# Token blocks of 144, 64 and 32 per weight quarter in a mixture-of-experts stage

## The reference, cut to what matters

```python
logits = jnp.einsum('btd,de->bte', h, router_w) + router_b
top_v, top_i = lax.top_k(logits, TOP_K)                # 2 of 8 experts
gates = jax.nn.softmax(top_v, axis=-1)
for e in range(N_EXPERTS):                             # D = 1024, expert width 3584
    y = y + combine[..., e:e+1] * (silu(h @ wg[e]) * (h @ wu[e])) @ wd[e]
```

## Time and profile before

| | |
|---|---|
| median of 3 runs | 2012.54 us (2012.41 to 2013.05) |
| profiled execution | 2011.59 us, of it 2009.7 us span |
| TensorE busy | 88% of the span |
| mean granted TensorE clock | 0.91 |
| SyncE's DMA queue | 65.1% of 16 engines' span |

### The profile page before, as it was taken

One profiled execution on the slowest core, in us unless ns is written; L12 is line 12 of the kernel. 1 busy time (PEld: TensorE's weight loads), 2 busy tenths in 40 slices (PEclk: granted clock), 3 DMA queues, 4 the chain that ended last, 5 costly groups with the idle time before them and its releaser, 6 DMA issues.

```text
span 2009.7 us, 27189 instructions
## 1 busy us (share of the span) xinstructions
PE 1771.1 (88%) x10676; PEld 1294.9 (64%) x10677; DVE 429.1 (21%) x810; ACT 241.5 (12%) x489; POOL 168.4 (8%) x204
## 2 busy tenths in 40 slices
PE   6999875566789999967889999999999999999874
PEld 3766443555567777745339689788777887778331
DVE  2023436764211111375000000000000000000102
ACT  2122342111110000132000000001000010000101
POOL 4002204562000000040000000000000000000001
PEclk8998597666889999977999999999999999999997
DMA  9762041001745554530898878879999999999995
GB/s 345 268 228 88 2 127 56 1 1 27 261 156 210 209 189 158 191 133 2 312 391 327 302 252 319 299 255 354 363 345 345 347 348 352 343 348 364 371 392 206
DMA packets 233583, 481.58 MB, mean 240 GB/s; under 512 B 14383, under 2 KB 89011, under 8 KB 233123
## 3 DMA queue, kind: packets, MB, share of 16 engines
q1 hardware_dynamic: 228027, 471.85, 65.1%
q0 software_dynamic: 3920, 5.44, 0.9%
q10 hardware_dynamic: 1568, 3.34, 0.5%
HBM read 473.06 MB, written 7.90 MB: 239 GB/s over the span
## 4 chain that ended last, share of the span: by engine, by line
PE 78%; DMA 6%; DVE 6%; POOL 4%; issue 3%; ACT 2%; SPq 1%; ACTq 0%; POOLq 0%; DVEq 0%
PE bank L1108 76%; DMA ring<-in_moe_w_up 4%; POOL ring L2305 2%; DMA ring<-in_ada_w 1%; POOL other L2317 1%; ACT ring L1590 1%; DVE wide L1882 1%; SPq L2396 0%; DVE wide L1866 0%; PE bank L1241 0%; DVE wide L2208 0%; SPq L2423 0%; PE bank L714 0%; DMA ring<-in_cache_fox_logf 0%; PE bank L1366 0%
## 5 line engine op out<-in xcount | busy, mean ns | idle before, releaser
L1108 PE MATMUL bank<-wide,ring 128*128 128x144 f32 (+4 forms) x4240 | 695.5, 331 | 16.6 <-DVE wide L1878 9.3
L1108 PEld LDWEIGHTS bank<-wide,ring 128*128 128x128 f32 (+2 forms) x4240 | 616.1, 190 | 100.6 <-issue 32.5
L1108 PE MATMUL bank<-ring 128*64 128x512 f32 (+8 forms) x1748 | 340.5, 521 | 50.1 <-DMA ring<-in_moe_w_up 24.1
L1108 PE MATMUL bank<-other,ring 128*128 128x144 f32 (+3 forms) x2016 | 291.4, 319 | 53.5 <-POOL ring L2305 31.1
L1108 PEld LDWEIGHTS bank<-other,ring 128*128 128x128 f32 (+1 forms) x2016 | 267.1, 192 | 78.2 <-POOL ring L2305 32.4
L1108 PEld LDWEIGHTS bank<-ring 128*64 128x64 f32 (+4 forms) x1748 | 144.7, 158 | 225.4 <-issue 188.4
L1108 PE MATMUL bank<-ring,other 128*64 128x512 f32 x560 | 128.0, 596 | 8.4 <-ACT other L747 8.4
L820 DVE TENSOR_TENSOR other<-other,bank 64x512 f32<-64x512 f32 (+1 forms) x40 | 24.5, 613 | 442.1 <-ACT other L744 442.1
L838 DVE TENSOR_TENSOR other<-other,bank 128x288 f32<-128x288 f32 (+3 forms) x48 | 21.4, 446 | 350.9 <-PE bank L1108 324.6
L2375 POOL TENSOR_TENSOR small<-const 128x1 f32<-128x1 f32 x1 | 0.2, 193 | 1075.8 <-DMA expert_rows<-ring 1075.8
L1108 PEld LDWEIGHTS bank<-ring,other 128*64 128x64 f32 x560 | 38.4, 137 | 75.4 <-issue 64.3
(11 more groups left out here) (354 smaller groups left out, 961.6 us busy)
## 6 DMA issues: line engine op xcount, KB each, us to landing
ring<-in_moe_w_gate SPq DMA_DIRECT2D x32, 2048.0 KB, 7.9
ring<-in_moe_w_up SPq DMA_DIRECT2D x32, 2048.0 KB, 12.7
ring<-in_moe_w_down SPq DMA_DIRECT2D x32, 2048.0 KB, 16.9
ring<-in_ada_w SPq DMA_DIRECT2D x24, 2048.0 KB, 13.5
ring<-in_moe_w_gate SPq DMA_DIRECT2D x32, 1536.0 KB, 11.1
ring<-in_moe_w_up SPq DMA_DIRECT2D x32, 1536.0 KB, 14.8
ring<-in_moe_w_down SPq DMA_DIRECT2D x32, 1536.0 KB, 16.5
ring<-in_w_in SPq DMA_DIRECT2D x5, 2048.0 KB, 12.6
```

Of the source, the lines that this page charges most:

```text
L1108: return pe.matmul(out, lhsT, rhs, start=start, stop=stop, skip_group_check=True)
```

## The change

- **Blocks.** An expert of up to 240 tokens (`CAP`) is cut into at most three blocks: one of 144 if it has over 96, one of 64 if over 32 remain, one of 32 for what is then left. Here: expert 2 is 144 + 32, expert 3 is 144, expert 4 is 64 + 32, expert 1 is 32, and 0, 5, 6, 7 are 64 each. The 192-wide form is gone. All blocks of an expert use one and the same loaded weight quarter.
- **Turns.** The plan has one word per quarter of an expert (a turn, `TURNS` = 40, of them 32 alive). Every engine loops over turns in batches of eight, reads the word and branches to the blocks. Waits count blocks (`b`), so a place is free for the next turn when the last block of this one is done with it.
- **The 32-token block.** Four column groups of 32: up and gate of part 0 in groups 0 and 1, then up and gate of part 1 in groups 2 and 3; then all seven transposes, then down over all four groups.
- **Pairs.** Now heavies are paired with experts of up to 96 tokens; the order of experts comes out as before.
- **Tokens** are copied by ScalarE per block and turn. **Rows** of a heavy expert are transposed in its own last turn. **Stores** move to GpSimd's queue. Of expert 0 only the first quarter is issued ahead of the plan.
- **Planner.** `moe_plan` has 19 small vector operations more and, for the turns, 11 operations on 40 x 10 elements; `moe_orders` (18 operations without data) runs ahead of the router's result.

```diff
-CAP, MID, HALF = 192, 144, 64
+MID, HALF, QUART = 144, 64, 32
+CAP, LIGHT = MID + HALF + QUART, HALF + QUART
...
+        def quarter_block(pe, mm, R, b):
...
+            pe.wait_ge(s("xe_ready"), b + 1)
+            pe.wait_ge(*after("moe_act", 5 * b - 2))
+            for part in range(2):
+                w = P * PARTS[part][1]
+                for kind in ("gate", "up"):
+                    pe.wait_ge(loaded(kind, part), 16 * R + 16)
+                for c in range(DC):
+                    for half, kind in enumerate(("up", "gate")):
+                        m = mm(B[0][group(2 * part + half), 0:w], xe_quart[:, c, :], moe_tile(kind, part)[:, c, :], c == 0, c == DC - 1)
+                        if c == DC - 1:
+                            m.then_inc(s(f"moe_{kind}"), 2)
+            pe.wait_ge(*after("moe_act", 5 * b + 3))
+            for part, (j0, n) in enumerate(PARTS):
+                o = group(2 * part)
+                for j in range(n):
+                    m = mm(B[TURN + part][:, QUART * j:QUART * (j + 1)], ea[o, part, P * j:P * (j + 1)], ident[o, o], True, True)
+                m.then_inc(s("moe_turn"), 1)
+            pe.wait_ge(*after("moe_silu", 6 * b + 6))
+            for part, (j0, n) in enumerate(PARTS):
+                pe.wait_ge(loaded("down", part), 16 * R + 16)
+                w = moe_tile("down", part)
+                for j in range(n):
+                    for p in range(2):
+                        m = mm(B[TURN + 1][group(2 * (j % 2) + p), :], eaT_few[:, j0 + j, 0:QUART], w[:, j, 512 * p:512 * (p + 1)],
+                               j0 + j < 2, j0 + j >= SUBS - 2)
...
+            act.wait_ge(*after("moe_up", 4 * b))
+            act.activation(xe_quart, xall[:, :, bass.ds(at, QUART)], ACT.Copy).then_inc(s("xe_ready"), 1)
...
-                    sp.wait_ge(*after("moe_down", 2 * R - 1 + part))
+                    sp.wait_ge(*after("moe_down", 2 * b - 1 + part))
                 else:
-                    sp.wait_ge(*after(f"moe_{kind}", 4 * R - 2 + 2 * part))
+                    sp.wait_ge(*after(f"moe_{kind}", 4 * b - 2 + 2 * part))
...
+            def turn(R):
+                big, half, quarter, last, b, heavy = plan_word(pe, BLOCKS, R, HAS + [LAST, AT, HEAVY])
+                with pe.If(big > 0):
+                    wide_block(pe, mm, R, b, heavy)
+                with pe.If(half > 0):
+                    half_block(pe, mm, R, pe.snap(b + big, min_val=0, max_val=255))
+                with pe.If(quarter > 0):
+                    quarter_block(pe, mm, R, pe.snap(b + big + half, min_val=0, max_val=255))
+                with pe.If(big + last > 1):
+                    wide_rows(pe, heavy, b + big + half + quarter)
...
+            def by_turn(out, value):
+                do(TT(by_seq, at_seq, spread(value, 1, TURNS), ALU.mult))
+                do(dve.tensor_reduce(out, by_seq, AX.X, ALU.add))
...
         def moe_sync(sp):
-            for r in range(ROUNDS):
-                moe_round(sp, r, r, 0, first=r == 0)
+            moe_round(sp, 0, 0, 0, first=True)
             sp.wait_ge(*once("planned"))
```

More of the change, by code:

```diff
@@ L726, in take_tokens @@
[L726 to L735, removed]
@@ L737, in scalar_light, with plan_word @@
-        def scalar_light(act, R):
+            pe.wait_ge(*after("out_act", 3 * heavy + 3))
+            pe.wait_ge(*after("out_dve", 3 * heavy + 3))
+        def plan_word(engine, row, R, fields):
+            word = engine.value_load(plan[0:1, bass.ds(R + row * NPLAN, 1)], min_val=0, max_val=2 ** 21 - 1)
+            return [engine.snap((word >> field[0]) & field[1], min_val=0, max_val=field[-1]) for field in fields]
+        HAS = [(0, 1), (1, 1), (2, 1)]
+        FIRST, LAST, ODD, AT, HEAVY, STORED = (3, 1), (4, 1), (5, 1), (6, 127), (13, 7), (16, 31)
@@ L757, in scalar_heavy, with scalar_turns @@
                 act.activation(sg[:, p % 2, 0:w], B[2 * (p % 2)][:, 0:w], ACT.Silu).then_inc(s("moe_silu"), 3 if p == 3 else 1)
-        def scalar_items(act):
+        def scalar_turns(act):
             B = banks.tiles
[L762 to L772, removed]
+            def turn(R):
+                big, half, quarter, last, b, heavy = plan_word(act, BLOCKS, R, HAS + [LAST, AT, HEAVY])
+                at, = [act.value_load(plan[0:1, bass.ds(R + COL * NPLAN, 1)], min_val=0, max_val=2 * N)]
+                half_at = act.snap(at + big * MID, min_val=0, max_val=2 * N + MID)
+                quarter_at = act.snap(half_at + half * HALF, min_val=0, max_val=2 * N + MID + HALF)
+                with act.If(big > 0):
+                    scalar_wide(act, b, at)
+                    with act.If(last > 0):
+                        for j in range(2):
+                            act.wait_ge(s("moe_acc"), 3 * b + 1 + j)
+                            act.activation(outT[:, 2 * j:2 * j + 2, :], B[ACC + j][:, 0:2 * MID].rearrange("p (c q) -> p c q", c=2),
+                                           ACT.Copy).then_inc(s("out_act"), 1)
+                with act.If(half > 0):
+                    scalar_half(act, act.snap(b + big, min_val=0, max_val=255), half_at)
+                with act.If(quarter > 0):
+                    scalar_quarter(act, act.snap(b + big + half, min_val=0, max_val=255), quarter_at)
+                with act.If(big + last > 1):
+                    act.wait_ge(*after("wide_out", 32 * heavy))
@@ L1014, in moe_plan @@
             do(TT(first_row, first_row, load, ALU.subtract))
-            do(TS(kind_of, load, float(HALF), 1.0, ALU.is_gt, ALU.add))
-            do(STT(kind_of, load, float(MID), kind_of, ALU.is_gt, ALU.add))
-            do(STT(kind_of[:, NE:ITEMS], load[:, NE:ITEMS], 0.0, kind_of[:, NE:ITEMS], ALU.is_gt, ALU.mult))
-            slot_kind, slot_light, seq, hseq, heavies = (slot_of[:, row, :] for row in range(5))
-            places = K("iota")[:, 0:ITEMS]
-            do(TS(paired, K("pairing"), pairs, None, ALU.is_lt))
@@ L1036, in moe_plan @@
-            do(STT(planf[:, WORD, 0:ITEMS], heavies, 256.0, slot_kind, ALU.mult, ALU.add))
-            do(dve.tensor_copy(planf[:, EXPERT, 0:ITEMS], got[:, 0, :]))
-            do(TT(planf[:, COL, 0:ITEMS], got[:, 2, :], begins, ALU.add))
-            do(dve.tensor_copy(planf[:, ROW, 0:ITEMS], first_row))
-            do(TS(planf[:, ROW, ITEMS:], ordinal[:, NE - 1:NE], float(NE), None, ALU.add))
-            do(dve.tensor_copy(plan[:, 0:4 * NPLAN], planf[0:1, :, :].rearrange("p a b -> p (a b)")), once.give("planned"))
+            big, half, quarter = (has[:, i, :] for i in range(3))
```

477 lines of the change are left out of this document (274 added, 203 removed).

## The result

The changed kernel takes 2109.28 us (median of 4 runs, 2107.98 to 2110.15), the kernel before 2012.47 (4 runs, 2010.95 to 2013.05): ratio 1.0482, 95% interval 1.0464 to 1.0500. The profiled execution took 2108.76 us, of it 2107.1 us span, against 2011.59 and 2009.7; the mean granted clock is 0.897 (0.910 before).

A forecast was written before the change was run, and what follows sets the result against it. It took TensorE to bound the pairs before and late-freed tile places the two-block turns after. Mixture 72.8, plan 10.8, start 1 and end 1 add 85.6 us to 2011.59: 2097, median 2098; range 2075 to 2125, 8 in 10 2058 to 2138.

The forecast's parts named there:

- The tiles: Turns with two blocks: next loads start only after the small block's first part; periods 86.1 and 72.6 us.
- the pause: Turns of experts 2 and 1 and of 4 and 6: no DMA traffic for some 20 us in each.
- its own sign against it: Mixture stage: the prediction is wrong if loads run on during the 144-wide block.
- the other sign: Mixture stage: the prediction is wrong if waits of TensorE named issue stand in every turn.
- Part 0: First gate and up products of the 32-token block: 32 records in 7.0 us, bounds 3.6 and 10.1.
- Rival 1: 32-token block's first gate and up products: four groups overlap, 3.6 instead of 7.0 us, 27 us less, 2071; chance 8%.
- The 32-token block: TensorE's small block: 12.2 + 1.7 + 1.9 + 0.4 + 3.2 = 19.4 us.
- a jump of 2.8 to new code: Before the first release in expert 2: TensorE's first jump to other code costs 2.8 us.
- The plan: VectorE's planning ahead of the second gather: 19 x 0.21 + 11 x 0.62 = 10.8 us longer, bounds 8 and 14.
- The mis-sized term: Experts 3 and 5: 4 x 0.4 us for ScalarE's copy each turn and 5.0 for rows; predicted difference +6.6.
- Rival 4: Each turn's jumps cost TensorE 2.79 us again, at 16 places: 42 us more, 2140; chance 8%.
- The sum: Whole kernel: 72.8 + 10.8 + 1 + 1 = 85.6 us on 2011.59, giving 2097; median 2098.

The follow-up runs named there:

- thinned pair: Changed kernel and kernel before, both with each weight load after the first ones cut to its tile's first chunk: 2005.90 us and 1973.36 us.

## Why the prediction was right, and where it was off

**The tiles: right, in mechanism and size.** From the release to the tile 41.7 us was predicted: 1118.0 to 1159.8 is 41.8. The period of experts 2 and 1 was to be 86.1 us and is 86.2, that of 4 and 6 72.6 and is 72.0; the loads stand still before each release. The two stages with two blocks in a turn (second and fourth lines of the table) are met to a microsecond, and the thinned pair shows that the cause is the tiles. The prediction put the pause too broadly, and its own sign against it (loads during the 144-wide block) did appear: they run on for some 17 us of that block, as its sum implies (56.4 - 41.7 = 14.7 us are left for that time). The pause is some 27 us in the turns of 2 and 1 and 14 in those of 4 and 6 (1772 to 1786), where 20 was said. Expert 6's block waits too (3.34 and 1.34 us, at 1799.25 and 1807.68), where one wait a turn was named. Waits named issue, the other sign, stand in the turns of experts 3 and 5 and behind rows, not in every turn.

**Part 0: right.** 32 records in 7.06 us, against 7.0. Rival 1 is out for this order of products, though not for the block: issued alternately over four groups they do overlap (7.06 us for all 64).

**The 32-token block: 17.2 us instead of 19.4.** Gate and up take 10.54 us and not 12.2 when all tiles are there, the stall 1.44 instead of 1.7, the transposes 1.32 instead of 1.9, down 3.63 (over 5 where the granted clock was low) instead of 3.2. In the periods none of it showed, since these pieces lie between waits for tiles. The stage of experts 0, 2 and 1 came out to the microsecond by errors that cancelled. From expert 0's first product to the first release it took 153.5 us (154.2 predicted, with a jump of 2.8 to new code that is not there: 1111.01 follows at once), the three periods 258.8 (258.3), the rest of the block 10.2 (12.4), and expert 2's rows 8.4 (1387.05 to 1395.42, 6.0 predicted):

```profile
1389.41 1.96 PE L763 MATMUL bank<-const,wide 128*128 128x128 f32 x16 [2.36 <-DVE ring L892]
1395.42 12.00 PE L1225 MATMUL bank<-ring 128*32 128x512 f32 x64 [4.05 <-issue]
```

**The plan: right.** VectorE's timeline, then TensorE's (the earlier trace rows before):

```profile
929.14 0.58 DVE L1139 TENSOR_TENSOR ring<-low,const 128x400 f32<-128x400 f32 x1
929.75 0.57 DVE L1142 TENSOR_TENSOR ring<-ring,low 128x400 f32<-128x400 f32 x1
```

```profile
942.86 14.06 PE L1225 MATMUL bank<-other 128*128 128x288 f32 x46 [1.06 <-DVE wide L1199]
964.60 10.66 PE L1225 MATMUL bank<-ring 128*64 128x512 f32 x41 [7.68 <-issue]
```

An operation of 400 elements starts 0.61 us after the last (0.62 predicted); the second gather is 10.85 us later (10.8 predicted). The start after it costs nothing: 7.68 us against 7.65, where I took 1.

**The mis-sized term: control in the turns of experts 3 and 5.** I priced it as 4 x 0.4 us, by ScalarE's copy against the cover that TensorE's last products give it, and 5.0 for rows; the stage measured 20.0 us longer against 6.6. It has two parts that the prediction did not hold. TensorE's issue stands 1.64 to 1.67 us between the large block and the 64-token one, which are now two turns with a plan word each where they were one round. And ScalarE needs 2.3 to 3.3 us of control ahead of its copy, where I took 1.72 from a transition between items, so TensorE waits 0.87 us, and 1.87 at a border of eight turns. With that the three full turns take 66.3, 65.8 and 66.5 us; in the first of them is also a wait of 1.24 us for a tile, in the third a slower restart (29.37 instead of 27.70). The last, 70.1 us, adds 2.0 for rows, 4.26 of issue behind them and a slower restart (12.64 instead of 10.96). Rival 4 named jumps as a price of every turn; it had the place right for these two experts and the size wrong (2.79 at 16 places), and behind the small blocks no such gap shows (1111.88 and 1129.08 above). Why it shows behind the 144-wide block and not behind them was not settled. The Trainium skill (Advanced Engine Details and Errata, Control Flow Timing) gives about 108 ns for a compare with branch; five of them (three blocks and the rows skipped or entered, and the loop) would be 0.54 us, an estimate. The runs show more: some 0.45 us for each block skipped, and 0.65 for a read.

**The sum.** 2108.76 in the profiled execution against 2097: 13.4 us too little in experts 3 and 5, 1.9 us too much in start and end.

## What to carry to other kernels

With one buffer per tile, look at who uses the tile last before you add a second user: the load of the next one starts there, and a long block in front of it then hides little. No run here gives a tile a second place. A stage that is bound by the columns of one block is helped by fitting its width (192 to 176: 0.65% faster), while cutting it into blocks paid only in columns saved, and with tiles free it saved none in the pair of experts 2 and 1 (75.9 us against 75.6). In a loop that runs on a plan word, price the read and the branches at every border of two turns, for the engine that is the bound and for the one that feeds it.

## What was not expected of the hardware

- Column groups overlap by the order of issue: two groups in alternation, twice, take 7.06 + 5.35 us when they wait between; back to back 10.54; four groups in alternation 7.06 for the same 64 records. The Trainium skill (TensorEngine Tiling (Array Packing), Theoretical Speedup) says up to four times for a dimension of 32 or less. From two groups to four the runs agree with it (221 to 110 ns a record, a factor of 2); that the order of issue decides is what the runs add, and no run shows one group alone.
- The same 28 down products of a small block took 3.63 us in one place and 5.32 in another, by the granted clock of their stretch: windows of the changed kernel,

```profile
1124.60:1130.00 5.40, 5.32 (x28) 1.25 (x28) 0.00 (x0) 0.43 (x2) 0.00 (x0) 0.68 1.04 386
1297.00:1302.40 5.40, 3.63 (x28) 0.91 (x28) 1.03 (x2) 0.45 (x2) 0.00 (x0) 1.00 1.05 387
```

In both blocks TensorE waited 1.44 and 0.34 us on either side of the transposes, and those ran at 1.00 (1123.00 to 1124.60, 1295.40 to 1297.00); what made the clock fall in the one and not in the other these rows do not tell. It costs nothing here, since a wait for a tile follows.
